# Loading and multiplying the first weight piece of a two-block network in three parts, with matmuls of ones ahead of it

## The reference

```python
for i in range(DEPTH):                       # DEPTH = 2
    z = x @ w_in[i]
    k, v = jnp.split(mem @ w_kv[i], 2, -1)   # layer 0: the first product of the kernel is k
    q = z[..., -MIX_WIDTH:]                  # the second product is q
    s = softmax(q k^T / sqrt(128)); xa = s v
    x = layer_norm(ALPHA * x + concat(tok, xa) @ w_out[i])
    f = grouped_moe(x, ...)                  # router picks one group of 4 experts, 2 experts in it
    x = layer_norm(ALPHA * x + f)
x = second_block(x, ...)                     # attention, forget-gate attention, a recurrent scan
```

## Time and profile before

| | |
|---|---|
| executions | 1476.21, 1476.27, 1480.7 us; median 1476.27 us |
| profiled execution: span, first to last instruction | 1475.1 us (what lies around the span is not recorded for it; the median stands 1.2 us above the span) |
| PE busy | 1404.1 us, 95% |
| DVE / ACT / POOL busy | 801.6 / 568.3 / 52.3 us |
| chain that ended last | PE 79%, DVE 8%, ACT 7%, DMA 3% |
| first matmul | 12.72 us after the first instruction |
| mean granted TensorE clock | 0.994 |

### The profile page before, as it was taken

One profiled execution on the slowest core, in us unless ns is written; L12 is line 12 of the kernel. 1 busy time (PEld: TensorE's weight loads), 2 busy tenths in 40 slices (PEclk: granted clock), 3 DMA queues, 4 the chain that ended last, 5 costly groups with the idle time before them and its releaser, 6 DMA issues.

```text
span 1475.1 us, 24626 instructions
## 1 busy us (share of the span) xinstructions
PE 1404.1 (95%) x10704; PEld 1015.7 (69%) x10704; DVE 801.6 (54%) x1186; ACT 568.3 (39%) x848; POOL 52.3 (4%) x43
## 2 busy tenths in 40 slices
PE   6999999999899999999899999988999999998898
PEld 6887454453796445444688787777788978877876
DVE  4766112211756121122777877677767886767764
ACT  4542111111442101111456476633546556764342
POOL 0010000000120000000000000010000000001000
PEclk9999999999999999999999999999999999999999
DMA  9448999999269999998344334410464433432032
GB/s 378 163 146 343 423 423 421 423 422 419 102 239 372 375 422 422 422 423 374 120 160 141 117 127 143 166 38 3 156 217 165 144 112 135 168 111 90 4 115 86
DMA packets 47490, 340.26 MB, mean 231 GB/s; under 512 B 5296, under 2 KB 5296, under 8 KB 7568
## 3 DMA queue, kind: packets, MB, share of 16 engines
q1 hardware_dynamic: 45504, 328.03, 57.3%
q0 software_dynamic: 1872, 10.57, 1.9%
HBM read 337.53 MB, written 1.05 MB: 230 GB/s over the span
## 4 chain that ended last, share of the span: by engine, by line
PE 79%; DVE 8%; ACT 7%; DMA 3%; issue 2%; DVEq 0%; SPq 0%
PE bank L541 47%; PE bank L904 14%; PE bank L945 7%; PE bank L848 4%; PE bank L547 3%; DMA ring<-wfirst 2%; ACT arena L1620 2%; ACT d_hi L1436 2%; DVE d_lo L1840 1%; ACT arena L1397 1%; PE bank L877 1%; PE bank L882 1%; DVE arena L2266 1%; DMA ring<-wsecond 1%; DVE arena L2415 1%
## 5 line engine op out<-in xcount | busy, mean ns | idle before, releaser
L1840 DVE TENSOR_TENSOR d_lo<-ring,d_hi 128x2048 fp32r<-128x2048 f32 (+2 forms) x111 | 249.3, 2255 | 110.7 <-ACT d_hi L1436 110.5
L1436 ACT ACTIVATE d_hi<-ring 128x2048 fp32r<-128x2048 f32 (+2 forms) x115 | 215.9, 1887 | 145.5 <-PE bank L541 114.8
L541 PE MATMUL bank<-arena 64*64 64x64 f32 (+7 forms) x3680 | 181.7, 235 | 20.0 <-ACT arena L1397 5.5
L541 PEld LDWEIGHTS bank<-arena 64*64 64x64 f32 (+4 forms) x3680 | 150.4, 139 | 47.1 <-issue 18.2
L1397 ACT ACTIVATE arena<-bank 128x512 f32<-128x512 f32 (+4 forms) x190 | 103.3, 552 | 188.4 <-PE bank L541 143.9
L541 PE MATMUL bank<-xT_hi,d_hi 128*128 128x256 f32 x592 | 167.3, 283 | 2.3 <-ACT arena L1716 1.7
L541 PE MATMUL bank<-xT_hi,d_lo 128*128 128x256 f32 x592 | 166.2, 281 | 0.0
L541 PE MATMUL bank<-d_hi,xT_hi 128*128 128x512 f32 (+1 forms) x400 | 158.9, 397 | 7.5 <-ACT arena L1658 4.0
L541 PE MATMUL bank<-xT_lo,d_hi 128*128 128x256 f32 x592 | 165.7, 280 | 0.0
L541 PE MATMUL bank<-d_hi,xT_lo 128*128 128x512 f32 (+1 forms) x400 | 158.1, 395 | 0.0
L541 PE MATMUL bank<-d_lo,xT_hi 128*128 128x512 f32 (+1 forms) x400 | 157.2, 393 | 0.0
(11 more groups left out here) (357 smaller groups left out, 2013.6 us busy)
## 6 DMA issues: line engine op xcount, KB each, us to landing
ring<-wmoe SPq DMA_DIRECT2D x84, 1024.0 KB, 17.7
ring<-wsecond SPq DMA_DIRECT2D x80, 1024.0 KB, 4.8
arena<-wmoe SPq DMA_DIRECT2D x72, 1024.0 KB, 18.1
ring<-wfirst SPq DMA_DIRECT2D x30, 1024.0 KB, 4.9
wide<-wmoe SPq DMA_DIRECT2D x24, 1024.0 KB, 20.2
xT_raw<-wmoe SPq DMA_DIRECT2D x12, 1024.0 KB, 20.5
rows<-lnrows POOLq DMA_DIRECT2D x4, 1024.0 KB, 7.4
ring<-wsecond SPq DMA_DIRECT2D x4, 848.0 KB, 10.7
```

Of the source, the lines that this page charges most:

```text
L541: mark(nc.tensor.matmul(o, lhsT, rhs, start=start, stop=stop, skip_group_check=loose), full)
L1436: nc.scalar.activation(high_of(u)[:, 0:width], raw[u % NRAW][:, 0:width], ACT.Copy).then_inc(sem("piece_high"), 1)
L1840: v.tensor_tensor(d_lo[u % NRAW][:, 0:width], raw[u % NRAW][:, 0:width], high_of(u)[:, 0:width], SUB).then_inc(sem("piece_low"), 1)
```

## The change

The load, the rounding and the multiplying of mem^T and piece 0 are each cut into three parts, of 2, 2 and 4 k-slices (`PARTS`). SP issues six loads in turns (mem^T part, piece part) of 256, 256, 256, 256, 512 and 512 KB where it issued two of 1 MB. ACT and DVE have three pairs of instructions where they had two instructions each. PE runs a new function `first_part`: the same 48 matmuls of piece 0 into bank 0, with k-slices 0 and 1 of both tiles first, then 2 and 3, then 4 to 7. Each group waits for its part. `proj_T` starts at part 1 for `kvk0`.

Ahead of it, DVE sets a 128x512 stretch of the arena to ones, and PE multiplies it with itself three times into bank 4, which nobody reads then.

The three routing signals become one semaphore, `routed`, that counts to 3 in each layer; the DVE instructions and their order stay.

```diff
+        PARTS = [(slice(k, end), slice(k * T, end * T)) for k, end in ((0, 2), (2, 4), (4, KD))]
+        warm = arena[:, xsc_at:xsc_at + 512]
...
-            sp.dma_start(memT_raw, memT0).then_inc(sem("memT_loaded"), 16)
-            at = 0
+            for q, (ks, cols) in enumerate(PARTS):
+                end = q + 1 == len(PARTS)
+                sp.dma_start(memT_raw[:, ks, :], memT0[:, ks, :]).then_inc(sem("memT_loaded" if end else f"part_loaded{q}"), 16)
+                sp.dma_start(raw[0][:, cols], wfirst0[:, cols]).then_inc(sem("piece_raw0" if end else f"part_loaded{q}"), 16)
+            n, at = 1, PROJ
...
+            def first_part():
+
+                hi, lo = v3(high_of(0), KD), v3(d_lo[0], KD)
+                pe_eng.wait_ge(bank_free[0], pe.reuse(0))
+                for q, (ks, _) in enumerate(PARTS):
+                    if q + 1 < len(PARTS):
+                        pe_eng.wait_ge(sem("memT_split"), 2 * q + 2)
+                    else:
+                        pe_eng.wait_ge(sem("memT_split"), 2 * q + 1)
+                        pe_eng.wait_ge(sem("piece_low"), 1)
+                    for m in range(2):
+                        cols, o = slice(m * P, (m + 1) * P), banks[0][:, m * T:(m + 1) * T]
+                        for k in range(ks.start, ks.stop):
+                            end = k == KD - 1
+                            mm(o, hi[:, k, cols], memT_hi[:, k, :], start=k == 0 and m == 0, stop=False, loose=True)
+                            mm(o, hi[:, k, cols], memT_lo[:, k, :], start=False, stop=False, loose=True)
+                            mm(o, lo[:, k, cols], memT_hi[:, k, :], start=False, stop=end, full=0 if end and m else None, loose=True)
+                pe.slots, pe.open = 1, 1
...
-            pe_eng.wait_ge(sem("memT_split"), 1)
+            pe_eng.wait_ge(dve_step, 1)
+            pe_eng.wait_ge(bank_free[4], pe.used(4))
+            for _ in range(3):
+                mm(banks[4][:, :], warm[:, 0:P], warm)
             for i in range(DEPTH):
                 if i == 0:
-                    proj_T("kvk0", memT, (0, 5))
+                    first_part()
+                    proj_T("kvk0", memT, (0, 5), first=1)
...
-                            pe_eng.wait_ge(sem("slots_ready"), i + 1)
+                            pe_eng.wait_ge(sem("routed"), 3 * i + 1)
...
+                nc.scalar.activation(memT_hi[:, ks, :], memT_raw[:, ks, :], ACT.Copy).then_inc(sem("memT_high"), 1)
+                if end:
+                    act_eng.wait_ge(sem("piece_raw0"), 16)
+                nc.scalar.activation(high_of(0)[:, cols], raw[0][:, cols], ACT.Copy).then_inc(sem("piece_high" if end else "memT_high"), 1)
+            act.pieces = 1
...
+            v.memset(warm, 1.0).then_inc(dve_step, dve.sends(dve_step))
+            for q, (ks, cols) in enumerate(PARTS):
+                end = q + 1 == len(PARTS)
+                dve_eng.wait_ge(sem("memT_high"), 2 * q + 1)
+                v.tensor_tensor(memT_lo[:, ks, :], memT_raw[:, ks, :], memT_hi[:, ks, :], SUB).then_inc(sem("memT_split"), 1)
```

More of the change, by code:

```diff
@@ L468, in load @@
                 return at + width
-            sp.dma_start(memT_raw, memT0).then_inc(sem("memT_loaded"), 16)
-            at = 0
+            for q, (ks, cols) in enumerate(PARTS):
[3 more added lines that the diff above has]
+            n, at = 1, PROJ
             for i in range(DEPTH):
-                for u in range(FIRST_PIECES[i] - (2 if i else 0)):
+                for u in range(FIRST_PIECES[i] - (2 if i else 1)):
                     at = load((wfirst0, wfirst1)[i], at)
@@ L639, in three_T, with proj_T @@
                 mm(o, w[1], x[0], start=False, stop=last, full=full)
-            def proj_T(name, rhsT, bs, tiles=4, between=None):
-                for part in range(-(-tiles // 2)):
+            def first_part():
[15 more added lines that the diff above has]
+                pe.slots, pe.open = 1, 1
+            def proj_T(name, rhsT, bs, tiles=4, between=None, first=0):
+                for part in range(first, -(-tiles // 2)):
                     n = min(2, tiles - 2 * part)
@@ L839, in gather @@
                         else:
-                            pe_eng.wait_ge(sem("picks_ready"), i + 1)
+                            pe_eng.wait_ge(sem("routed"), 3 * i + 3)
                             pe_eng.wait_ge(sem("tokens_first"), g)
@@ L854, in gather @@
                     if p == 0:
-                        pe_eng.wait_ge(sem("comb_ready"), i + 1)
+                        pe_eng.wait_ge(sem("routed"), 3 * i + 2)
                     else:
@@ L1444, in tok_high @@
                 nc.scalar.activation(catT_hi[:, 4 * i:4 * i + 4, :], uT, ACT.Copy).then_inc(sem("tok_high"), 1)
-            act_eng.wait_ge(sem("memT_loaded"), 16)
-            nc.scalar.activation(memT_hi, memT_raw, ACT.Copy).then_inc(sem("memT_high"), 1)
+            for q, (ks, cols) in enumerate(PARTS):
+                end = q + 1 == len(PARTS)
+                if end:
+                    act_eng.wait_ge(sem("memT_loaded"), 16)
+                else:
+                    act_eng.wait_ge(sem(f"part_loaded{q}"), 32)
+                nc.scalar.activation(memT_hi[:, ks, :], memT_raw[:, ks, :], ACT.Copy).then_inc(sem("memT_high"), 1)
+                if end:
+                    act_eng.wait_ge(sem("piece_raw0"), 16)
+                nc.scalar.activation(high_of(0)[:, cols], raw[0][:, cols], ACT.Copy).then_inc(sem("piece_high" if end else "memT_high"), 1)
+            act.pieces = 1
             for i in range(DEPTH):
@@ L1913, in rms_second @@
                 rms_scale(l, 1)
-            dve_eng.wait_ge(sem("memT_high"), 1)
-            v.tensor_tensor(memT_lo, memT_raw, memT_hi, SUB).then_inc(sem("memT_split"), 1)
+            v.memset(warm, 1.0).then_inc(dve_step, dve.sends(dve_step))
+            for q, (ks, cols) in enumerate(PARTS):
+                end = q + 1 == len(PARTS)
+                dve_eng.wait_ge(sem("memT_high"), 2 * q + 1)
+                v.tensor_tensor(memT_lo[:, ks, :], memT_raw[:, ks, :], memT_hi[:, ks, :], SUB).then_inc(sem("memT_split"), 1)
+                if end:
+                    dve_eng.wait_ge(sem("piece_high"), 1)
+                else:
+                    dve_eng.wait_ge(sem("memT_high"), 2 * q + 2)
+                v.tensor_tensor(d_lo[0][:, cols], raw[0][:, cols], high_of(0)[:, cols], SUB).then_inc(sem("piece_low" if end else "memT_split"), 1)
+            dve.pieces = 1
             for i in range(DEPTH):
@@ L2088, in picks @@
                     return ins
[L2090 to L2092 removed]
+                picks(0, 2).then_inc(sem("routed"), dve.sends(sem("routed")))
+                v.tensor_tensor(v3(S_COMB, TT), v3(S_COMB, TT), per_channel(S_RS[:, 0:TT], NE), MUL).then_inc(sem("routed"), dve.sends(sem("routed")))
+                picks(2, NE).then_inc(sem("routed"), dve.sends(sem("routed")))
                 v.tensor_reduce(S_MX[:, 0:1], S_CNT, AX, ADD).then_inc(dve_step, dve.sends(dve_step))
```

## The result

The changed kernel takes 1481.56 us in the median of 12 executions, beside 1477.22 for the kernel before: the ratio is 1.0029, 95% interval 1.0016 to 1.0043, or +2.4 to +6.4 us. Medians are those of executions in the fast state: one of e14 (1604.96 us), one of e15 (2033.49) and one of before (7756.69) in the last measurement were slow and are left out. The prediction was 1477.8 with a range up to 1480.6: slower was right, 1.5 us was not. (It started from three executions of before with a median of 1476.27; all twelve have 1477.22.) From one execution to the next both kernels vary by several us (1475.2 to 1480.7 before, 1477.7 to 1487.9 now); the profiled one (1485.6 us, 4 above its median) has a span of 1483.4 us, 8.3 more than before. So the trace is read stretch by stretch, and not by its span.

The account below looks back on a forecast made before the run. It took PE to bound the kernel (busy 95% of the span, 79% of the chain). Piece 1's start, -0.25 us, and the low clock, +1.75, gave +1.5: from 1476.27 to 1477.8, range 1475.0 to 1480.6.

Parts of the forecast that it names:

- How late x^T is: Step on the x^T load queued behind the six cut loads: taken as 0.3 us late, at most 2.7.
- the slack: At piece 1's start on PE: it could have begun at 19.9 instead of 20.45, 0.55 us.
- Rival 3: First loads: short runs slow the stream, piece 1 comes 2.7 us late, +3.9 in all, 1480.2; chance 0.07.
- The clock term: In piece 1 on PE: the low clock rate returns behind 4 to 6 us of idle time, costing 1.75 us.
- the two terms: Piece 1's start on PE, 0.25 us won, and the low clock rate in piece 1, 1.75 us lost.
- Rival 2: At piece 1: it is cut before x^T arrives, PE starts it 5.1 us early, 1471.2; chance 0.03.
- not needed until far behind q0: Piece 4's load, issued on piece 1's first matmul: 0.25 us earlier, but claimed to be needed only much later.

Follow-up runs that it names:

- e14: The changed kernel measured a second time, unaltered: 1483.5 us beside 1477.7 for the kernel before, ratio 1.0030.
- e15: The changed kernel with six more matmuls of ones between piece 0 and piece 1: 1479.1 us beside 1477.7 before, ratio 1.0004.
- e2: The changed kernel with piece 1 rounded and cut ahead of x^T on ACT and DVE: 1480.6 us beside 1477.7 before, ratio 1.0006.
- e3: The changed kernel with piece 1 ahead of x^T, two parts (four 512 KB loads) and five matmuls of ones: 1479.1 us beside 1477.7 before, ratio 1.0010.
- e9: The changed kernel without the three matmuls of ones and their constants: 1480.7 us beside 1478.2 before, ratio 1.0017.
- e8: The kernel before with only the routing signals made one count: 1476.3 us beside 1477.5 before, ratio 0.9991.
- e6: The kernel before with only the six cut loads, ACT waiting for five of them: 1480.0 us beside 1477.7 before, ratio 1.0009.
- e7: The kernel before with mem^T and piece 0 in sixteen loads of 128 KB: 1483.1 us in one execution, beside 1478.2 before.
- e4: The changed kernel with whole 1 MB loads and piece 1 ahead of x^T: 1478.2 us beside 1478.2 before, ratio 1.0004.
- e16: The changed kernel with whole loads, piece 1 ahead of x^T and q0's banks emptied before piece 4 is cut: 1475.6 us beside 1477.7 before, ratio 0.9984.

## Why the prediction was wrong

**The place and the mechanism were right.** It said that piece 1, behind x^T on ACT and DVE, decides; that PE would stand idle ahead of it; and that the clock would come back low in piece 1. All three are in the trace, e2 shows the first by moving piece 1 (3.9 us earlier), and e15 the last by filling the idle time.

**The step that failed is "How late x^T is".** It took 0.3 us. It is 2.25 and 2.0 us in the two traces of the changed kernel. The 0.3 came from a subtraction, 4.8 us for 1 MB less 3.5 for 512 KB, "512 KB in 1.3 us, 403 GB/s". In such a difference whatever a load costs beside its bytes drops out, and that was the cost: about 0.4 us for each load more. Its other premise, that the stream doesn't run dry because an issue of 0.45 us is shorter than 256 KB, is contradicted too, by 270 and 328 GB/s. Of the lateness 0.55 was covered by the slack, as said. So piece 1 starts 1.66 and 1.44 late instead of 0.25 early.

**Rival 3 had nearly the right number for the wrong reason.** It put +3.9 on the case that short runs are slow, with a chance of 0.07. Two more loads, with half-long runs, should have cost 0.2 us by it (0.1 on 1 MB), and they cost 0.77 (e3). Its 2.7 us was the upper bound of a cost that no row showed, and giving it 7% because one row looked friendly was the error of the chances. The Trainium skill ("DMA: Bandwidth & Descriptors", section "Measured (HBM→SBUF, 128 partitions, SWDGE, issued from GpSimd)") wants 1 MB and more in one load; the estimate of 1.2 us that the prediction made from its figure came nearer than the 0.3, and the 239 to 270 GB/s of the cut loads in these traces speak for its rule, while the 423 to 426 GB/s of queued 1 MB loads are above its 341.

**The clock term, 1.75 us, had about the right size.** From piece 1's start to the scores the first trace loses 3.04 - 1.66 = 1.4, the second 4.27 - 1.44 = 2.8, e9's 2.1. The low rate covered 2.9 and 6.1 us of busy time, in the second case more than the 3.4 or 4.5 of the rows.

**Sum:** the two terms make 3.0 and 4.3 at the scores, where +1.5 was forecast; measured were +4.3 and +5.9 in the medians, each some 2 us uncertain. The prediction has no term for the 1.3 to 1.6 us between them; it says of the matmuls of ones that they delay nothing, and looks at the start alone. The load behind 1132 that is 1.5 us late in both traces, and on time in every trace without ones, would fill it; that the ones are its cause is the likely reading and not isolated.

**Rival 2 was rightly small for this kernel**, but "I see nothing else for it" hid the next wait: even with piece 1 early (e2), 2.4 of 3.9 us were gone at the scores, where PE waited for DVE. The prediction's "not needed until far behind q0", said of piece 4, was wrong for DVE, which cuts it before it empties q0's banks.

**The rest.** First product 7.02 (6.6), ones from 1.72 in 5.49 us (4.2 to 5.1), third part 13.09 (11.0, late by the same loads). The fillers delayed nothing at the start (the first product is at 7.02 in e9 too) and helped nothing at piece 1. That the routing signals cost nothing was not contradicted by e8.

## What to carry to other kernels

Ahead of cutting a first load to start earlier, find what the second product waits for: here it hung on a load behind the cut ones, so the early start turned into idle time and the cut made that load late. Price a cut by the number of loads that it adds as well as by their bytes, and look at what is queued behind the wait on *every* engine in order, since the next one (here piece 4 ahead of q0's copies) takes the gain back. Idle time of PE just before dense work can cost twice; if it can't be removed, matmuls that nobody reads belong into exactly that gap: there they won 4.5 us back (e15), while the same matmuls ahead of an idle time gained nothing and seem to have cost over 1 us far behind.

## What the runs showed of the hardware

- In a queue of 128-row loads each further load delayed what was behind by 0.37 to 0.39 us in e3, e6 and e7 (0.34 to 0.56 in the six traces with three parts), for sizes of 128 to 512 KB. From 2.5 to 5.0 us the rate was 377 GB/s with 1 MB loads (before), 270 with 256 KB (changed) and 239 with 128 KB (e7).
- A packet took 309 ns for 8 KB, 159 for 4 KB, 84 for 2 KB and 46 for 1 KB (medians, before, e3, changed, e7).
- The clock can stay low while PE looks busy: 13.7 us at half in e4, where PE was busy for 12.46 of 13.70 us with small matmuls. PE had been 4.5 us ahead of the kernel before up to this stretch and was 0.9 behind after it.
- A dozen executions of one kernel differed by 4.7 (e8) to 13.2 us (e16), so that a gain of 3 us is only just seen in them.
- A 1 MB load was on ACT 4.74 to 4.89 us after its issue in nine traces, and 5.07 to 7.13 in the eight in which a 16 KB "instruction" packet started between 0.03 us before and 0.64 behind this issue.
